# Where TensorE's operands begin in SBUF: a two-block transformer forward pass, dense activations placed 256 bytes past the weights

## The chip, the cores and the metric

The kernel runs on one core of one Trainium2 chip. The metric is the device time of one execution in microseconds. Three executions of the kernel before took 2189.39, 2189.68 and 2189.95 us, so the median is 2189.68 us.

## What is computed

Two blocks, one after the other, on 256 tokens of width 1024, all in float32. The first has two layers (a mixer with four branches, then a dense SwiGLU in layer 0 and a mixture of eight experts in layer 1). The second has two hybrid layers (retention, a state-space mixer, stick-breaking attention, a memory read). What matters for the change is the matrix products, which are nearly all of TensorE's work:

```python
z = rms_norm(h, norm1_g) @ w_in[layer]            # 256x1024 @ 1024x7168, cut into branches and gates
merged = sum(gates[i] * (y[i] @ w_branch[i]) for i in range(4))
h = h + merged @ w_out[layer]
h = h + (silu(g) * u) @ w_down                    # layer 0: g, u = hn @ w_gate_up (d_ff 2816)
h = h + sum(combine[:, e] * swiglu(hn, w_gate_up[e], w_down[e]) for e in range(8))   # layer 1: d_ff 3584
# second block, per layer
proj = rmsnorm(x, pre_g) @ w_in_2[l]              # 1024 x 6664
kv = rmsnorm(mem, mem_norm_g) @ w_mem_kv[l]
x = x + rmsnorm(concat([y_ret, y_ssd, y_sb, y_mem]) @ w_out_2[l], post_g)
```

## The kernel before, in words

Every large product is made of three products in a rounded float32 format (fp32r). Weights and activations are each split into a high part (a rounded copy, made by ScalarE) and a low part (the remainder, made by VectorE). TensorE adds up activation-high x weight-high, activation-low x weight-high and activation-high x weight-low in one PSUM bank.

A TensorE product takes two instructions. LDWEIGHTS loads one operand into the array, always 128 columns wide here (8 for one narrow tile). MATMUL then streams the other operand past it, 512 or 256 columns wide. In this text they are the loaded and the streamed operand. TensorE starts the LDWEIGHTS of the next product while the present one streams.

The SBUF tensors that the products read:

- `ring`: 5 x 16 KB per partition. In the dense stages it is used as nine half tiles (`halves_r`) of 8 KB for weights, with `xT_low` in the last 8 KB. In the expert stage it holds five tiles of expert weights, and their low parts are written over them (`w_low`).
- `xT` / `xT_high`, `xT_low`: the transposed, normalised activations, eight chunks of 128 rows x 256 tokens. In the expert stage `xg_high`, the 128 tokens gathered for an expert, lies in `xT`'s memory.
- `arena`: one large tensor that three sets of views cut up in turn (`Views` objects A and B for the first block, E for the experts, C for the second block). In it lie `w_high`, `hid_high`, `hid_low`, `xg_low`, `hidT_*`, the branch outputs `ya_*` to `yd_*`, and in the second block `mg*`, the memory's activations, and `yT_high`, `yr_low`, `yd_low`, `ys_low`.

`weigh` (in the TensorE program) issues a dense product tile by tile. Its two forms are `rows` (L908), which loads 128 tokens of the activations and streams 512 columns of weights (256 in a few tiles), and `cols` (L914), which loads 128 columns of weights and streams 256 tokens:

```python
return pe.matmul(o[:, a:a + n], x[:, c, b * P:(b + 1) * P], w[:, k, col:col + n], **flags)   # L908, rows
return pe.matmul(o[:, a:a + SEQ], w[:, k, j * P:(j + 1) * P], x[:, c, :], **flags)           # L914, cols
```

The first of the two tensors is the loaded one. In a high half it alternates `high` and `low` activations; in the low half it takes `high` alone. The experts (L1169, L1170, L1173 for the up products, L1210, L1212, L1217 for the down products) load activations and stream 512 columns of `w_high` or `w_low`. L1147 and L1148 put an expert's last rows back. L955 transposes 128x128 blocks with the identity in `consts`. L1244 is the narrow tile: it loads 8 columns of weights and streams 256 tokens.

All chunks, blocks and column groups of these tensors are steps of 512 bytes or multiples of it (128 floats), the narrow tile's 32-byte steps excepted. So the place of an operand within 512 bytes is the place of its tensor's start, whichever chunk is read.

The order of the work is written out by hand in each engine's program. SyncE loads weights in the order in which TensorE needs them: each load waits until TensorE has finished with the piece of the ring that it overwrites (L827 for dense halves, L818 for expert tiles).

Of the kernel before, what the change touches and what calls it, by code (L numbers as in the profile page):

```python
# [17 lines left out]
P = 128  # L18
SEQ, D = 256, 1024
TB = SEQ // P  # L20
KC = D // P
# [34 lines left out]
NRAW, NTOP = 5, 4  # L56
RAW_AT, TOP_AT = (6, 7, 2, 3, 4), (5, 0, 1, 8)
HALF = 2048
# [306 lines left out]
def kernel_program(nc, t):  # L365
# [28 lines left out]
    with ctx:  # L394
        def sb(name, shape, dt=F32):
            return ctx.enter_context(nc.sbuf_tensor(name, shape, dt))
# [4 lines left out]
        def placed(name, shape, dt=F32):  # L401

            at = -(-nc.sbuf_base // 32) * 32
            return sb(name, shape, dt), at

        def rounded(name, shape, at):

            return nc.alloc_sbuf_tensor_at(name, [P, *shape], F32R, offset=at)


        ring, ring_at = placed("ring", [P, NSLOT, TILE])
        raw = ring[:, :, :].rearrange("p a b -> p (a b)")
        halves_r = rounded("halves_r", [NRAW + NTOP, HALF], ring_at)
        xT_low = rounded("xT_low", [KC, SEQ], ring_at + 4 * (NRAW + NTOP) * HALF)
        h = sb("h", [P, TB, D])
        xs, xs_at = placed("xs", [P, TB, D])
        ym_low = rounded("ym_low", [4, SEQ], xs_at + 4 * D)
        xT, xT_at = placed("xT", [P, KC, SEQ])
        xT_high = rounded("xT_high", [KC, SEQ], xT_at)
        consts = sb("consts", [P, 7, P])  # L420
        ident, flip, le, lt, ge, ones, slots_row = (consts[:, k, :] for k in range(7))
        ssq = sb("ssq", [P, 8])
        rstd = sb("rstd", [P, 8])
        par_all = sb("par_all", [P, LAYERS, 80])
        ARENA = 25400
        arena, arena_at = placed("arena", [P, ARENA])

        class Views:


            def __init__(self, at=0):
                self.at = at

            def __call__(self, *shape):
                n = math.prod(shape)
                v = arena[:, self.at:self.at + n]
                self.at += n
                assert self.at <= ARENA, self.at
                return shaped(v, *shape)

        def shaped(v, *shape):
            if len(shape) == 1:
                return v
            names = "abcd"[:len(shape)]
            return v.rearrange(f"p ({' '.join(names)}) -> p {' '.join(names)}",
                               **{k: s for k, s in zip(names[1:], shape[1:])})
# [23 lines left out]
        A = Views()  # L470
# [31 lines left out]
        branch_top = rounded("branch_top", [2 * WIDE], arena_at + 4 * A.at)  # L502
        sguT = A(4, P)
        zT = A(2, SEQ + 2)
        A(4)
        q_n = A(TB, ATTN)
        yd_high = rounded("yd_high", [HEADS, SEQ], arena_at + 4 * A.at)
        k_n = A(TB, ATTN)
# [53 lines left out]
        xg_high = rounded("xg_high", [KC, P], xT_at)  # L562
        rt = Views(ARENA - 256)(256)
        lt_r, ones_r, chosen_r = xg_low[:, 0, :], xg_low[:, 1, :], xg_low[:, 2, 0:2 * EXPERTS]
        flag_word = rt[0:1, 200:201].bitcast(I32)
        token_ids = rounded("token_ids", [TB, 8], arena_at + 4 * (ARENA - 256 + 176))
        next_rows = rt[:, 192:193].bitcast(U32)
# [3 lines left out]
        C = Views()  # L571
        mask_strict, mask_incl = C(TRI), C(TRI)
        rope_c, rope_s = C(TB, P), C(TB, P)
        decay = C(4, TRI)
        par = C(96)
        post_row = C(D)
        ssd_row = C(512)
        kmT = C(4, SEQ)
# [4 lines left out]
        gm = C(TB, 512)  # L583
        mg1_high = [rounded(f"mg1_high_{'ab'[k]}", [KC // 2, SEQ], arena_at + 4 * (C.at + k * KC // 2 * SEQ)) for k in range(2)]
        xbc = C(8, SEQ + 4)
        yd_low = rounded("yd_low", [4, SEQ], arena_at + 4 * C.at)
        xz = C(2 * TB, 512)
        xh, zs = xz[:, 0:TB, :], xz[:, TB:2 * TB, :]
# [10 lines left out]
        small2 = C(256)  # L599
        assert E.at <= ARENA - 256 and C.at <= E.at - 2 * KC * P  # L600

# [2454 lines left out]
```

## Time and profile before

| what | value |
|---|---|
| median of three runs | 2189.68 us |
| span of the profiled execution | 2188.4 us |
| time outside the span (median less span) | 1.3 us |
| TensorE MATMUL busy | 2150.1 us, 98% |
| LDWEIGHTS busy | 1812.1 us, 83% |
| VectorE, ScalarE, GpSimd busy | 73%, 61%, 4% |
| granted TensorE clock, mean | 0.996 of full speed |
| chain that ended last | TensorE 90%, VectorE 4%, DMA 3%, ScalarE 2% |

The span is the profiler's; no time of its own is known for the profiled execution beyond it, so its 2188.4 us stands beside the median. MATMULs overlap: the mean duration of one (some 390 ns for 512 columns) is longer than the step from one start to the next. The step is what costs time, and it is read from the chain of work: a piece of the chain with x48 matmuls in 10.91 us has a step of 10.91/48 = 227.3 ns.

### The profile page before, as it was taken

The numbers are of one execution on the slowest core, as the hardware profiler recorded it, in microseconds if no ns is written. First come the engines' busy times: TensorE is split into PE (matmuls) and PEld (weight loads), VectorE is DVE, ScalarE is ACT, GpSimd is POOL, SyncE is SP. The second block draws the span as 40 slices with busy tenths as digits, with TensorE's granted clock in tenths as the row PEclk, the third lists the DMA queues.
The fourth block names the chain that finished last, engine by engine and source line by source line (L and its number), as shares of the span: only waits on it lengthen the run. The fifth ranks groups of instructions, "written<-read, shape, count | busy, mean of one in ns | idle before, by whom it ended". The sixth has DMA issues, their size and how long they took to land.

```text
span 2188.4 us, 27831 instructions
## 1 busy us (share of the span) xinstructions
PE 2150.1 (98%) x10935; PEld 1812.1 (83%) x10935; DVE 1592.3 (73%) x1339; ACT 1331.8 (61%) x1151; POOL 78.0 (4%) x67
## 2 busy tenths in 40 slices
PE   7999999999998999999999999999999999999998
PEld 6988788888787888888888888888888898899987
DVE  5576555466766888888888888888896667565665
ACT  4475544455656677776777777777675555456542
POOL 3100000000000000000000000000110000000000
PEclk9999999999998999999999999999999999999999
DMA  8554565554538999999999999999996534455442
GB/s 279 156 191 147 208 201 177 183 183 155 198 139 310 335 383 375 370 375 372 386 364 381 375 377 365 382 375 370 384 374 225 173 117 153 157 178 173 134 154 77
DMA packets 249166, 569.70 MB, mean 260 GB/s; under 512 B 12169, under 2 KB 14353, under 8 KB 248817
## 3 DMA queue, kind: packets, MB, share of 16 engines
q1 hardware_dynamic: 242368, 546.41, 69.8%
q0 software_dynamic: 5136, 16.70, 2.3%
q10 hardware_dynamic: 1568, 5.31, 0.6%
q8 instruction: 64, 1.05, 0.2%
q14 instruction: 30, 0.24, 0.0%
HBM read 562.60 MB, written 5.78 MB: 260 GB/s over the span
## 4 chain that ended last, share of the span: by engine, by line
PE 90%; DVE 4%; DMA 3%; ACT 2%; issue 0%; SPq 0%; DVEq 0%; ACTq 0%
PE bank L908 32%; PE bank L1169 9%; PE bank L1170 9%; PE bank L1173 9%; PE bank L914 9%; PE bank L1217 5%; PE bank L1210 5%; PE bank L1212 5%; PE bank L955 3%; DMA ring<-w_in 2%; DVE halves_r L2185 1%; DMA ring<-moe_w_down 1%; ACT halves_r L1663 1%; DVE w_low L2613 0%; DMA ring<-w_out 0%
## 5 line engine op out<-in xcount | busy, mean ns | idle before, releaser
L2613 DVE TENSOR_TENSOR w_low<-ring,w_high 128x4096 fp32r<-128x4096 f32 x167 | 736.3, 4421 | 75.8 <-ACT w_high L1892 75.1
L1892 ACT ACTIVATE w_high<-ring 128x4096 fp32r<-128x4096 f32 x167 | 606.8, 3634 | 236.5 <-DMA ring<-moe_w_gate_up 141.4
L908 PE MATMUL bank<-halves_r,xT_high 128*128 128x512 f32 (+1 forms) x1856 | 563.3, 381 | 6.1 <-ACT halves_r L1663 3.1
L2185 DVE TENSOR_TENSOR halves_r<-ring,halves_r 128x2048 fp32r<-128x2048 f32 x175 | 391.6, 2265 | 162.2 <-ACT halves_r L1663 160.0
L908 PEld LDWEIGHTS bank<-halves_r,xT_high 128*128 128x128 f32 x1856 | 344.1, 189 | 73.8 <-issue 5.2
L1663 ACT ACTIVATE halves_r<-ring 128x2048 fp32r<-128x2048 f32 x175 | 326.2, 1891 | 118.7 <-DMA ring<-w_in 55.5
L1169 PE MATMUL bank<-w_high,xg_high 128*128 128x512 f32 x896 | 357.6, 399 | 1.7 <-DVE xg_low L2590 1.7
L1170 PE MATMUL bank<-w_high,xg_low 128*128 128x512 f32 x896 | 351.8, 393 | 0.0
L908 PE MATMUL bank<-halves_r,xT_low 128*128 128x512 f32 (+1 forms) x928 | 348.7, 380 | 0.0
L1173 PE MATMUL bank<-w_low,xg_high 128*128 128x512 f32 x896 | 224.3, 392 | 0.0
L908 PEld LDWEIGHTS bank<-halves_r,xT_low 128*128 128x128 f32 x928 | 175.3, 189 | 32.1
L1169 PEld LDWEIGHTS bank<-w_high,xg_high 128*128 128x128 f32 x896 | 168.3, 188 | 38.5 <-issue 1.9
L1173 PEld LDWEIGHTS bank<-w_low,xg_high 128*128 128x128 f32 x896 | 168.2, 188 | 37.9
L1170 PEld LDWEIGHTS bank<-w_high,xg_low 128*128 128x128 f32 x896 | 168.5, 188 | 35.8
L1210 PE MATMUL bank<-w_high,hid_high 128*128 128x512 f32 x448 | 176.6, 394 | 0.0
L1212 PE MATMUL bank<-w_high,hid_low 128*128 128x512 f32 x448 | 174.9, 390 | 0.0
L914 PE MATMUL bank<-xT_high,halves_r 128*128 128x256 f32 x896 | 165.1, 284 | 0.0
L1641 ACT ACTIVATE arena<-bank 128x512 f32<-128x512 f32 x82 | 47.4, 596 | 158.0 <-PE bank L914 82.3
L914 PEld LDWEIGHTS bank<-xT_high,halves_r 128*128 128x128 f32 x896 | 140.9, 192 | 0.9 <-issue 0.8
L1217 PE MATMUL bank<-w_low,hid_high 128*128 128x512 f32 x448 | 114.2, 394 | 0.4 <-DVE w_low L2613 0.4
L914 PE MATMUL bank<-xT_low,halves_r 128*128 128x256 f32 x448 | 108.8, 283 | 0.0
L1217 PEld LDWEIGHTS bank<-w_low,hid_high 128*128 128x128 f32 x448 | 84.0, 188 | 20.0 <-DVE w_low L2613 0.8
(392 smaller groups left out, 2312.7 us busy)
## 6 DMA issues: line engine op xcount, KB each, us to landing
ring<-moe_w_gate_up SPq DMA_DIRECT2D x224, 1024.0 KB, 10.4
ring<-moe_w_down SPq DMA_DIRECT2D x112, 1024.0 KB, 9.8
ring<-w_in SPq DMA_DIRECT2D x108, 1024.0 KB, 5.2
ring<-w_out SPq DMA_DIRECT2D x24, 1024.0 KB, 4.9
ring<-ffn_w_gate_up SPq DMA_DIRECT2D x22, 1024.0 KB, 5.3
ring<-ffn_w_down SPq DMA_DIRECT2D x11, 1024.0 KB, 4.8
ring<-w_mem_kv SPq DMA_DIRECT2D x8, 1024.0 KB, 5.1
ring<-w_branch_attn SPq DMA_DIRECT2D x4, 1024.0 KB, 5.1
```

Of the source, the lines that this page charges most:

```text
L908: return pe.matmul(o[:, a:a + n], x[:, c, b * P:(b + 1) * P], w[:, k, col:col + n], **flags)
L914: return pe.matmul(o[:, a:a + SEQ], w[:, k, j * P:(j + 1) * P], x[:, c, :], **flags)
L1169: pe.matmul(o[:, :], xg_high[:, c, :], w[:, c, :], start=c == 0, stop=False)
L1170: pe.matmul(o[:, :], xg_low[:, c, :], w[:, c, :], start=False, stop=False)
L1173: mm = pe.matmul(o[:, :], xg_high[:, c, :], w[:, c, :], start=False, stop=c == KC - 1)
L1210: pe.matmul(acc[n][:, :], hid_high[:, 4 * k + c, :], v[:, c, :], start=k + c == 0, stop=False)
L1212: pe.matmul(acc[n][:, :], hid_low[:, 4 * k + c, :], v[:, c, :], start=False, stop=False)
L1217: mm = pe.matmul(acc[n][:, :], hid_high[:, 4 * k + c, :], v[:, c, :], start=False, stop=4 * k + c == EX_CH - 1)
L1663: act.activation(top_view(half), raw_view(half), ACT.Copy).then_inc(top_in, 1)
L1892: act.activation(high_slot(k), ring[:, ring_r.slot(names[k]), :], ACT.Copy).then_inc(w_high_in[r], 1)
L2185: dve.tensor_tensor(raw_view(half, halves_r), raw_view(half), top_view(half).bitcast(F32), ALU.subtract).then_inc(raw_low_in, 1)
L2613: dve.tensor_tensor(w_low[:, slot, :], ring[:, slot, :], high_slot(k).bitcast(F32), ALU.subtract).then_inc(w_low_in[r], 1)
```

## The change

It changes where tensors begin in SBUF, and nothing else. Each engine issues the same instructions on the same shapes, in the same order and with the same waits as before; only addresses differ. The allocation order changes (the arena now comes before `ssq`, `rstd` and `par_all`), two fillers of 256 bytes are put in, the arena shrinks by 56 floats, and three views of the arena are rounded up to a multiple of 128 floats.

Start of each tensor in bytes, modulo 512:

| tensor | before | after |
|---|---|---|
| `halves_r`, `w_low` (ring), `consts` | 128 | 128 |
| `xT_low`, `xT_high`, `xg_high`, `xs`, `ym_low` | 128 | 384 |
| `w_high`, `hid_high`, `hid_low`, `xg_low`, `hidT_high`, `hidT_low` | 320 | 128 |
| `ya_*`, `yb_*`, `yc_*`, `branch_top` | 320 | 128 |
| `yd_high`, `yd_lower` (first block) | 352 | 128 |
| `mg*` of the second block's layer 0 / layer 1 | 320 / 192 | 128 |
| `yT_high`, `yr_low`, `yd_low`, `ys_low` | 320 | 128 |

The distance of a product is here the start of the operand that is being loaded less the start of the one that is being streamed, modulo 512. Distances, before and after:

| streamed, loaded during it | line | before | after |
|---|---|---|---|
| `halves_r`, `xT_*` | L908 | 0 | 256 |
| `xT_*`, `halves_r` | L914 | 0 | 256 |
| `halves_r`, `hidT_*`, `yT_high` and three of the four low parts of y | L908 | 192 | 0 |
| `halves_r`, `mg*` of layer 0 / 1 | L908 | 192 / 64 | 0 |
| `mg*` of layer 0 / 1, `halves_r` | L914 | 320 / 448 | 0 |
| `w_high`, `xg_low` | L1169 | 0 | 0 |
| `w_high`, `xg_high` | L1170 | 320 | 256 |
| `w_low`, `xg_high` | L1173 | 0 | 256 |
| `w_high`, `hid_*` | L1210, L1212 | 0 | 0 |
| `w_low`, `hid_high` | L1217 | 192 | 0 |

```diff
@@ -411,25 +411,32 @@
-        xT_low = rounded("xT_low", [KC, SEQ], ring_at + 4 * (NRAW + NTOP) * HALF)
+        xT_low = rounded("xT_low", [KC, SEQ], ring_at + 4 * (NRAW + NTOP) * HALF + 2 * P)
+        sb("xT_low_end", [P, P // 2])
...
         xT_high = rounded("xT_high", [KC, SEQ], xT_at)
+        sb("half_line", [P, P // 2])
         consts = sb("consts", [P, 7, P])
         ident, flip, le, lt, ge, ones, slots_row = (consts[:, k, :] for k in range(7))
+        ARENA = 25344
+        arena, arena_at = placed("arena", [P, ARENA])
         ssq = sb("ssq", [P, 8])
         rstd = sb("rstd", [P, 8])
         par_all = sb("par_all", [P, LAYERS, 80])
-        ARENA = 25400
-        arena, arena_at = placed("arena", [P, ARENA])
+        assert ring_at % (4 * P) == (xT_at + 2 * P) % (4 * P) == arena_at % (4 * P)
...
+            def line_up(self):
+
+                self.at = -(-self.at // P) * P
...
         zT = A(2, SEQ + 2)
-        A(4)
+        A.line_up()
         q_n = A(TB, ATTN)
...
         par = C(96)
+        C.line_up()
         post_row = C(D)
...
         xbc = C(8, SEQ + 4)
+        C.line_up()
         yd_low = rounded("yd_low", [4, SEQ], arena_at + 4 * C.at)
```

## Rows read from the trace of the kernel before

**Rows 1.** The page, part 1: busy time, share, instructions of TensorE's matmuls

```profile
PE 2150.1 (98%) x10935; PEld 1812.1 (83%) x10935; DVE 1592.3 (73%) x1339; ACT 1331.8 (61%) x1151; POOL 78.0 (4%) x67
```

**Rows 2.** The page, part 4: the chain that ended last, by engine

```profile
PE 90%; DVE 4%; DMA 3%; ACT 2%; issue 0%; SPq 0%; DVEq 0%; ACTq 0%
```

**Rows 3.** Waits of PE, longest; waits of SP on expert matmuls (us, times, longest)

```profile
PE bank L955 <- DVE xs L2170: 11.8, 4, 9.3
...
SPq L818 <- PE bank L1173: 506.1, 88, 15.5
...
SPq L818 <- PE bank L1217: 230.5, 44, 10.8
```

**Rows 4.** Windows: us, busy by engine with instructions, clock, DMA share, GB/s

```profile
1000.00:1300.00 300.00, 300.00 (x1353) 245.29 (x1352) 255.58 (x102) 219.92 (x103) 8.92 (x2) 1.00 0.99 374
1700.00:1950.00 250.00, 247.00 (x1485) 218.83 (x1484) 160.70 (x227) 133.65 (x190) 1.59 (x3) 1.00 0.49 161
```

**Rows 5.** Groups of instructions by line and shape: x count, busy us, mean ns

```profile
L908 PE MATMUL bank<-halves_r,xT_high 128*128 128x512 f32 x1664 | 526.8, 393 | 6.1 <-ACT halves_r L1663 3.1 <-DVE xT_low L2178 1.8 <-issue 0.9
L1169 PE MATMUL bank<-w_high,xg_high 128*128 128x512 f32 x896 | 357.6, 399 | 1.7 <-DVE xg_low L2590 1.7
...
L908 PE MATMUL bank<-halves_r,xT_low 128*128 128x512 f32 x832 | 325.3, 391 | 0.0
...
L1210 PE MATMUL bank<-w_high,hid_high 128*128 128x512 f32 x448 | 176.6, 394 | 0.0
...
L914 PE MATMUL bank<-xT_high,halves_r 128*128 128x256 f32 x896 | 165.1, 284 | 0.0
...
L914 PE MATMUL bank<-xT_low,halves_r 128*128 128x256 f32 x448 | 108.8, 283 | 0.0
...
L908 PE MATMUL bank<-halves_r,yT_high 128*128 128x512 f32 x256 | 81.5, 395 | 1.9 <-DVE yr_low L2798 1.9
...
L908 PE MATMUL bank<-halves_r,hidT_high 128*128 128x512 f32 x176 | 55.2, 392 | 0.0
...
L908 PE MATMUL bank<-halves_r,xT_high 128*128 128x256 f32 x192 | 36.6, 284 | 0.0
```

**Rows 6.** Timeline, expert stage: start us, us, engine (PEld is LDWEIGHTS)

```profile
1000.12 0.39 PE L1169 MATMUL bank<-w_high,xg_high 128*128 128x512 f32 x1
1000.12 0.19 PEld L1170 LDWEIGHTS bank<-w_high,xg_low 128*128 128x128 f32 x1
```

**Rows 7.** Chain pieces (start us, us, what), distance 0

```profile
307.82 21.81 PE bank L908 x96
...
463.57 10.91 PE bank L908 x48
...
1748.85 11.52 PE bank L914 x96
```

**Rows 8.** Chain pieces at other distances: hidT, then mg

```profile
387.90 46.72 PE bank L908 x204
...
1661.93 7.54 PE bank L914 x64
1669.47 5.60 PE bank L908 x24
...
1676.82 5.28 PE bank L908 x23
...
1931.70 5.60 PE bank L908 x24
```

**Rows 9.** Windows over two up tiles, then two down tiles, of one expert

```profile
998.88:1010.39 11.51, 11.51 (x54) 9.41 (x53) 9.96 (x4) 8.25 (x4) 0.00 (x0) 1.00 0.87 338
1010.39:1021.84 11.45, 11.45 (x54) 9.40 (x53) 11.34 (x6) 7.87 (x3) 0.00 (x0) 1.00 1.03 412
```

**Rows 10.** Chain pieces: the transposes inside one of these windows, the narrow tile

```profile
1004.43 0.44 PE bank L955 x4
...
1716.26 2.77 PE bank L1244 x24
```

## The prediction

> **What bounds the kernel now.** I read the busy shares first, then the chain that ended last, then TensorE's own waits. MATMULs are busy 2150.1 of 2188.4 us [rows 1], and the chain lies on TensorE for 90% [rows 2]. The longest wait of TensorE for anything is 11.8 us in total [rows 3], which is mostly the start of the program. So the time is the sum of the steps from one matmul to the next, about 10,900 of them, and an edit that moves no instruction can matter only through that step.
>
> The expert stage needs a second look, because the DMA engines are busy there too: share 0.99 at 374 GB/s, while TensorE has no idle microsecond in 300 [rows 4]. Who waits for whom settles it. SyncE's loads wait for expert matmuls to free a tile for 506.1 + 230.5 us [rows 3]. The loads are paced by TensorE there, not the other way round.
>
> **What the step depends on.** The granted clock is 1.00 in the windows read [rows 4], the 2.4 GHz level, at which 512 columns take 213.3 ns and 256 columns 106.7 ns. The steps are longer, and they differ with where the two operands begin:
>
> - distance 0, 512 columns: 21.81/96 = 227.2 ns and 10.91/48 = 227.3 ns; distance 0, 256 columns: 11.52/96 = 120.0 ns [rows 7]
> - distance 192, 512 columns: 46.72/204 = 229.0 ns in the down product of the dense SwiGLU; for the memory's activations 5.60/24 = 233.3 ns in one product and 5.28/23 = 229.6 ns in the next [rows 8]
> - distance 64, 512 columns: 5.60/24 = 233.3 ns, the piece at 1931.70 [rows 8]
> - distance 320, 256 columns: 7.54/64 = 117.8 ns [rows 8].
>
> The same instruction on the same shape thus takes 227 to 233 ns, depending on the place. A cause is at hand: the LDWEIGHTS of the next product starts with the MATMUL that is streaming (both at 1000.12) and runs 0.19 us of its step [rows 6]. It and the stream read SBUF side by side. The extra is 13.3 ns per product for 256 columns (120.0 less 106.7) and about 14 ns for 512, so it comes once per product and not per column, as it would if the load disturbs the stream.
>
> **The change part by part.** No engine gets an instruction more or less, nor a wait. There are three groups of products.
>
> *First, products that leave other distances for 0.* I price them at 227.3 ns, the step of 48 matmuls behind a break [rows 7].
>
> - Expert up products, 3 x 896 = 2688 (L1169, L1170 and L1173 have the same count [rows 5]). Two up tiles take 11.51 us less 0.44 for four transposes, over 48 matmuls: 230.6 ns [rows 9, 10]. Only a third of them (L1169) ends at distance 0, the rest at 256; see below.
> - Expert down products, 3 x 448 = 1344. Two tiles: (11.45 - 0.44)/48 = 229.4 ns [rows 9, 10]. At 227.3 they save 1344 x 2.1 = 2.8 us.
> - `yT_high` (256) with three low parts of 32 each, and `hidT` (176 high and half as many low): 352 + 264 = 616 at 229.0, saving 616 x 1.7 = 1.0 us [rows 5, 8].
> - `mg` under L908, 96 products, about three quarters of them at 233.3 and the rest at 229.6: 232.4 on the mean, saving 0.5 us. `mg` under L914, 192 products, goes the other way, from 117.8 to 120.0: plus 0.4 us [rows 7, 8].
>
> *Second, the dense products with `xT`*, which go from 0 to 256: 1664 + 832 = 2496 with 512 columns, and 896 + 448 + 192 + 96 = 1632 with 256 columns [rows 5] (the low half of the last pair has half the count of the high). No row shows distance 256. I bound it by the nearest rows. Above, 233.3 for 512 columns [rows 8] and 120.0 for 256 [rows 7]. Below, the narrow tile: 24 matmuls of 256 columns, at distances from 0 to 224 in steps of 32, take 2.77/24 = 115.4 ns with only 8 columns to load [rows 10]; that is 4.6 ns under 120.0, and I put the same 4.6 under 227.3 for a low end of 222.7. The clock allows no less than 106.7 and 213.3.
>
> I take no change for this group: 227.3 and 120.0. The reason is the pattern of the distances. 320 is 64 plus 256, and the distances 192 and 64, also 128 apart, share the value 233.3 [rows 8]. If the places repeat every 128 or 256 bytes, 256 is the same as 0.
>
> *Third, the two thirds of the expert up products that end at 256.* By the same assumption all 2688 fall from 230.6 to 227.3: 8.9 us.
>
> VectorE, ScalarE and the DMAs also read and write at new places. TensorE does not wait for them by more than a microsecond or two at a time, so a few nanoseconds per instruction stay hidden; if they grew until the experts' weights came late, a wait of TensorE on `w_low` would appear. The loads must run 230.6/227.3 = 1.4% faster in the up tiles, about 380 GB/s for 374, and a window here shows 412 [rows 4, 9].
>
> Sum: -8.9 - 2.8 - 1.0 - 0.5 + 0.4 = -12.8 us on a span of 2188.4, so 2175.6. The median lies 1.3 us above the span of the profiled execution, which makes 2176.9; I say 2177.
>
> **A rule against it.** The Trainium skill (TensorE: Matmul & The Clock Gate, Part 2, on LDWEIGHTS) says that TensorE has two independent SBUF read ports, so that loading the next weights takes no read bandwidth from the running matmul, and SBUF — State Buffer, in its summary of who contends, says TensorE never waits on anyone. By that rule placement does nothing and the sum is 0. The trace does not agree: one shape has steps of 227.3, 229.0 and 233.3 ns.
>
> **The rivals.**
>
> *A half-line distance frees the stream.* If the places repeat every 512 bytes, 256 is the farthest that two starts can be apart, and it may be better than 0. For it: 256 columns run faster at 320 (117.8) than at 0 (120.0). Against it: 512 columns do not, at 192 or 64. Price at the low ends: 2496 x 4.6 = 11.5 us, 1632 x 4.6 = 7.5 us, and 1792 expert products from 227.3 to 222.7, 8.2 us, beyond the 12.8: -40.0 us, 2149.7. At the clock's own floor it would be 34.9 + 21.7 + 25.1 us beyond it, 2095; the expert loads would then hardly keep up.
>
> *Distance 256 is one of the bad ones; slower.* The mechanism is that of the 233.3 ns products: the dense `rows` products (L908) leave the good distance 0. 2496 x 6.0 = +15.0 us; 1632 x -2.2 = -3.6 us; 1792 expert up products from 230.6 to 233.3, +4.8; the other 896 to 227.3, -3.0; the rest -3.9. Together +9.3 us, 2199.0. For it: every distance other than 0 that a row shows for 512 columns is worse than 0. Against it: none of those is 256. It decides from a step of about 231.1 ns for these 4288 products: there 2496 x 3.8 + 1792 x 0.5 = 10.4 us, which is what the other terms save. At 229.0, the commoner value of distance 192, the sum is still -9.2 us.
>
> *The start places do nothing.* The steps of 229 and 233 ns might come from what other engines and DMAs do in those stages, not from the place; the time would stay 2189.7. The rule of the Trainium skill above would end there too. For it: the slow up products stand where the DMA share is 0.99. Against it: the `mg` products of both layers repeat 5.60 us to the hundredth, 262 us apart, and the dense product at 387.90 holds 229.0 over 204 matmuls while its neighbours hold 227.2.
>
> **How the numbers follow.** The forecast (256 acts like 0, or near the 229.0 case) gets 0.42, the gain at half a line 0.27, the slower case 0.20, no effect 0.11. A measurement of this kernel can tell 0.2%, 4.4 us, from no change. Faster: 0.42 + 0.27, less a little for weak versions of the forecast that stay within 4.4 us: 0.67. Same: 0.13. Slower: 0.20. The likeliest case alone spans 2172 to 2183. For 8 in 10 the range must take in the middle of the half-line rival below and nearly all of the slower one above: 2146 to 2200.
>
> **What would show it.** In the changed profile, TensorE stays at 98% with the same 10,935 matmuls. Pieces of the chain over dense `rows` products of x48 should still take 10.91 us and `cols` of x96 11.52 us; 10.69 or less means the half-line rival, 11.2 the slower one. The `hidT` piece of x204 should fall from 46.72 to about 46.4 us. Two expert down tiles should take 11.35 us for 11.45. The forecast fails if the dense pieces move either way, since 4128 products depend on one distance that no row shows; it also fails if a wait of TensorE on `w_high` or `w_low` of more than 2 us in total turns up.

## The result, and the profile after

The changed kernel takes 2178.36 us (median of four, 2178.17 to 2178.79). The kernel before, run beside it on the same chip, takes 2189.81 us. The ratio is 0.9942, with a 95% interval from 0.9928 to 0.9955, so the kernel is 11.4 us or 0.6% faster. The forecast was 2177.0.

The page, parts 1 and 4, of the kernel after: busy time with share and instructions, then the chain that ended last by engine. It stands against [rows 1, 2].

```profile
PE 2137.2 (98%) x10935; PEld 1811.7 (83%) x10935; DVE 1591.8 (73%) x1339; ACT 1331.9 (61%) x1151; POOL 78.2 (4%) x67
...
PE 90%; DVE 4%; DMA 3%; ACT 2%; issue 0%; SPq 0%; DVEq 0%; ACTq 0%
```

The matmuls are busy for 12.9 us less with the same count, and no other engine's busy time moved by more than 0.5 us. The chain's shares are the same. The span fell by 11.8 us, from 2188.4 to 2176.6.

Waits in the kernel after: engine, line, what was waited for, us in total, times, longest. They stand against [rows 3].

```profile
PE bank L964 <- DVE xs L2179: 12.4, 4, 9.4
...
PE bank L1226 <- DVE w_low L2622: 0.6, 1, 0.6
...
SPq L827 <- PE bank L1182: 493.1, 88, 15.8
...
SPq L827 <- PE bank L1226: 228.9, 44, 11.3
```

TensorE's own long wait is 0.6 us longer, and its wait on expert weights is 0.6 us in all. SyncE's waits for the expert matmuls fell by 13.0 + 1.6 us, since TensorE frees the tiles earlier.

Windows of the kernel after: two up tiles, two down tiles, and 300 us of the expert stage, with the columns of [rows 4]. They stand against [rows 9] and the first line of [rows 4].

```profile
994.24:1005.61 11.37, 11.37 (x53) 9.40 (x53) 9.96 (x4) 8.33 (x4) 0.00 (x0) 1.00 0.92 346
1005.61:1016.98 11.37, 11.37 (x53) 9.42 (x53) 11.20 (x6) 7.89 (x3) 0.00 (x0) 1.00 1.03 415
1000.00:1300.00 300.00, 300.00 (x1367) 247.79 (x1366) 258.05 (x103) 222.65 (x104) 12.94 (x3) 1.00 1.01 378
```

In the same 300 us TensorE starts 1367 matmuls where it started 1353, that is 1.0% more, and the loads run at 378 GB/s for 374. Two tiles of 48 products with four transposes (0.44 us, as in [rows 10]) take 11.37 us: (11.37 - 0.44)/48 = 227.7 ns a step, for 230.6 and 229.4 before.

Pieces of the chain of the kernel after (start us, us, what), against [rows 7, 8, 10]: dense products with `xT` (twice x96), `hidT` (x204), `xT` again (x48), the `mg` products (from 1650.82 to 1665.71), the narrow tile (1705.11) and 256-column products with `xT` (1737.70).

```profile
306.82 21.78 PE bank L917 x96
329.48 21.81 PE bank L917 x96
386.78 46.30 PE bank L917 x204
462.31 10.93 PE bank L917 x48
...
1650.82 7.67 PE bank L923 x64
1658.50 5.47 PE bank L917 x24
...
1665.71 5.46 PE bank L917 x24
...
1705.11 2.77 PE bank L1253 x24
...
1737.70 11.52 PE bank L923 x96
```

The pieces that went from distance 0 to 256 did not move: 21.81 and 21.78 for 21.81, 10.93 for 10.91, 11.52 for 11.52. Those that went from another distance to 0 did: 46.72 to 46.30 over 204 products (229.0 to 227.0 ns), 5.60 to 5.47 over 24 (233.3 to 227.9), and, the other way, 7.54 to 7.67 over 64 products of 256 columns (117.8 to 119.8).

Added up over the whole trace by kind of product, the difference is as below. A step is the time from the start of one matmul to the start of the next and is counted for the first of the two. The sums are made from the records of both traces. The means leave out steps over 300 ns, which have a wait or transposes in them; the sums keep them.

| products | mean step before, ns | after | sum, us |
|---|---|---|---|
| up, `w_high` x `xg_high`, 896 | 231.7 | 227.9 | -3.10 |
| up, `w_high` x `xg_low`, 896 | 230.5 | 228.0 | -2.27 |
| up, `w_low` x `xg_high`, 896 | 230.0 | 227.0 | -2.66 |
| down, `w_low` x `hid_high`, 448 | 231.8 | 227.3 | -1.36 |
| down, the other 896 | 228.3 | 227.3 | -0.37 |
| `yT` with its low parts, `hidT`, `mg` rows, 712 | 229.3 | 227.1 | -1.53 |
| first block's `ya` to `yd`, 240 | 231.7 | 228.7 | -0.61 |
| `mg` cols, 192 of 256 columns | 126.1 | 128.1 | +0.24 |
| dense with `xT`, 2496 of 512 columns | 227.4 | 227.2 | -1.05 |
| everything else, transposes above all | | | +0.83 |

Together that is -11.9 us, and the span fell by 11.8. (The means of the `mg` cols have short breaks in them; inside their pieces the step goes from 117.8 to 120.0.)

The down products lost part of their gain again. Their steps under 300 ns alone save (231.8 - 227.3) x 444 = 2.0 us and 1.0 ns x 875 = 0.9 us. Of the steps over 300 ns there are 28 for 22, and they took 1.2 us more than the others' pace would give. One of the new ones took 230 ns before and takes 382 ns now. The timeline of the kernel after at that place (start us, us, engine, line, and in brackets the idle time ahead with its releaser):

```profile
1511.60 3.63 ACT L1901 ACTIVATE w_high<-ring 128x4096 fp32r<-128x4096 f32 x1 [0.89 <-DMA ring<-moe_w_gate_up]
...
1515.52 0.19 PEld L1219 LDWEIGHTS bank<-w_high,hid_high 128*128 128x128 f32 x1 [0.41 <-ACT w_high L1901]
1515.52 0.49 PE L1219 MATMUL bank<-w_high,hid_high 128*128 128x512 f32 x1
```

ScalarE waited 0.89 us for the weights from memory, its rounded copy came late, and the load that TensorE could have done beside the last stream had to wait for it. The faster matmuls have reached the weight stream at a few tiles.

The waits of TensorE's weight loads on the experts' rounded weights, before and then after (us in total, times, longest), show the same:

```profile
PEld bank L1210 <- ACT w_high L1892: 1.3, 5, 0.3
...
PEld bank L1217 <- DVE w_low L2613: 0.8, 1, 0.8
```

```profile
PEld bank L1219 <- ACT w_high L1901: 2.0, 6, 0.4
...
PEld bank L1226 <- DVE w_low L2622: 1.0, 1, 1.0
```

With one more of 0.2 us in the up products, these are 3.2 us after for 2.1 us before. Part of each is hidden under the stream of the product ahead.

### The profile page after: what moved, and what is told of

Its sections match the earlier page's. It is cut to its first block, busy times and chain, and to the rows that moved or that the text cites. A ratio compares the mean times of both kernels' runs of the same rounds, so it can differ in the third digit from the quotient of the medians.

```text
span 2176.6 us, 27831 instructions
## 1 busy us (share of the span) xinstructions
PE 2137.2 (98%) x10935; PEld 1811.7 (83%) x10935; DVE 1591.8 (73%) x1339; ACT 1331.9 (61%) x1151; POOL 78.2 (4%) x67
## 3 DMA queue, kind: packets, MB, share of 16 engines
q8 instruction: 64, 1.05, 0.2%
## 4 chain that ended last, share of the span: by engine, by line
PE 90%; DVE 4%; DMA 3%; ACT 2%; issue 0%; SPq 0%; DVEq 0%; ACTq 0%
PE bank L917 33%; PE bank L1178 9%; PE bank L1179 9%; PE bank L1182 9%; PE bank L923 9%; PE bank L1226 5%; PE bank L1219 5%; PE bank L1221 5%; PE bank L964 3%; DMA ring<-w_in 2%; DVE halves_r L2194 1%; DMA ring<-moe_w_down 1%; ACT halves_r L1672 1%; DVE w_low L2622 0%; DMA ring<-w_out 0%
## 5 line engine op out<-in xcount | busy, mean ns | idle before, releaser
L1672 ACT ACTIVATE halves_r<-ring 128x2048 fp32r<-128x2048 f32 x175 | 326.2, 1892 | 118.6 <-DMA ring<-w_in 57.4
L1219 PEld LDWEIGHTS bank<-w_high,hid_high 128*128 128x128 f32 x448 | 84.1, 188 | 19.2 <-ACT w_high L1901 2.0
## 6 DMA issues: line engine op xcount, KB each, us to landing
ring<-moe_w_gate_up SPq DMA_DIRECT2D x224, 1024.0 KB, 10.6
```

Source lines behind the costliest of these rows:

```text
L1219: pe.matmul(acc[n][:, :], hid_high[:, 4 * k + c, :], v[:, c, :], start=k + c == 0, stop=False)
L1672: act.activation(top_view(half), raw_view(half), ACT.Copy).then_inc(top_in, 1)
```

## The experiments

All kernels were run beside the kernel before, and each ratio is against that one. The edits are given against the kernel after, except that of `only_xt`, which is given against the kernel before; the changes to the closing assert that go with them are left out. The first four ask what the shift of `xT` by 256 bytes does, the next four give `xT` other distances, and the last three move all operands together, the arena alone, or `xT_low` alone.

**all_same: the activations at the same place as the weights.** No filler, so that every distance named in the table of the change is 0.

```diff
-        xT_low = rounded("xT_low", [KC, SEQ], ring_at + 4 * (NRAW + NTOP) * HALF + 2 * P)
-        sb("xT_low_end", [P, P // 2])
+        xT_low = rounded("xT_low", [KC, SEQ], ring_at + 4 * (NRAW + NTOP) * HALF + 0)
...
-        sb("half_line", [P, P // 2])
```

> All TensorE operands begin at the same place within 512 bytes: xT, xT_low and xg_high at distance 0 from the weights instead of 256, the arena lined up as in the changed kernel. Theory R (places repeat every 256 bytes or less, and the gain comes from the products that left 192, 320 and 64): the same time as the changed kernel, 2178.4 us within 1 us; dense 512-column pieces of x48 at 10.91 us, 256-column pieces of x96 at 11.52 us. Rival H (256 is itself a good distance and part of the gain hangs on it): slower than the changed kernel, by up to the 3.5 us that the xT products and the half of the up products reading xg_high contributed.

Measured: 2181.04 us (2180.28 to 2182.87), ratio 0.9958 (0.9942 to 0.9975). The span is 2178.0 us. Pieces of its chain: dense rows, `hidT`, dense cols.

```profile
283.86 21.77 PE bank L915 x96
...
386.47 46.30 PE bank L915 x204
...
1739.19 11.52 PE bank L921 x96
```

These are the pieces of the kernel after within 0.01 us. The medians differ by 2.7 us, but they come from different chips, so both kernels were timed again on one.

**after_again and all_same_again.** The two kernels unchanged, on one chip together.

> The changed kernel once more, beside all_same_again on one chip. If 0 and 256 are alike the two agree within 0.1%, 2 us; if 256 is the better of the two, this one is faster by 1 to 3 us, as the first pair of medians (2178.4 and 2181.0, on different chips) could suggest.

> All operands at distance 0, beside after_again: the same time within 2 us if 0 and 256 are alike; slower by 1 to 3 us if the half line is worth something of its own.

Measured: after 2179.03 us (2177.95 to 2182.61), ratio 0.9948 (0.9935 to 0.9962); all at the same place 2178.36 us (2177.36 to 2180.78), ratio 0.9944 (0.9930 to 0.9957). The 2.7 us are gone, and the sign with them. The shift by 256 bytes, which the change is named after, is worth nothing that these runs can tell from 0; lining up the rest, which is all that the kernel with everything at one place does, is worth all of it.

**only_xt: the shift alone.** Against the kernel before, with the arena's start where it was modulo 512 and no view rounded up.

```diff
-        xT_low = rounded("xT_low", [KC, SEQ], ring_at + 4 * (NRAW + NTOP) * HALF)
+        xT_low = rounded("xT_low", [KC, SEQ], ring_at + 4 * (NRAW + NTOP) * HALF + 2 * P)
+        sb("xT_low_end", [P, P // 2])
...
+        sb("half_line", [P, P // 2])
...
-        ARENA = 25400
+        ARENA = 25360
```

> The kernel before with one part of the change alone: xT, xT_low and xg_high moved from 0 to 256 bytes past the weights; the arena's tensors keep their places (320, 352, 192). Theory R: no change, 2189.8 us within 1 us, since 0 and 256 are alike, and so are 320 and 64 for L1170. Rival H: part or all of the 11.4 us is here, down to 2178 us.

Measured: 2190.23 us for 2190.28 before, ratio 1.0003 (0.9993 to 1.0012). Its chain and its window of the expert stage:

```profile
307.23 21.81 PE bank L910 x96
...
387.31 46.72 PE bank L910 x204
...
1747.91 11.52 PE bank L916 x96
```

```profile
1000.00:1300.00 300.00, 300.00 (x1353) 245.30 (x1352) 255.75 (x101) 219.93 (x103) 8.92 (x2) 1.00 0.99 374
```

All three pieces and the 1353 matmuls are those of before [rows 4, 7, 8]. Here the up products go from distance 320 to 64 and from 0 to 256, and the dense ones from 0 to 256; no step moves.

**xt_128: the activations 128 bytes on.** If the places repeated every 128 bytes, this would be the kernel after again.

```diff
-        xT_low = rounded("xT_low", [KC, SEQ], ring_at + 4 * (NRAW + NTOP) * HALF + 2 * P)
-        sb("xT_low_end", [P, P // 2])
+        xT_low = rounded("xT_low", [KC, SEQ], ring_at + 4 * (NRAW + NTOP) * HALF + 128)
+        sb("xT_low_end", [P, 32])
...
-        sb("half_line", [P, P // 2])
+        sb("half_line", [P, 96])
```

> As the changed kernel, but xT, xT_low and xg_high are 128 bytes past the weights instead of 256. If places repeat every 128 bytes: 2178.4 us within 1 us. If they repeat only every 256 bytes, 128 is a distance that no row has shown, and it may be as bad as 64: 2496 dense and 1792 expert products at 229.0 to 233.3 ns instead of 227.2, that is +8 to +26 us, less 3.6 us for 1632 products of 256 columns at 117.8 ns: 2183 to 2201 us.

Measured: 2201.03 us (2199.95 to 2202.58), ratio 1.0048 (1.0032 to 1.0065): 23 us above the kernel after. Dense rows, `hidT`, dense cols:

```profile
287.26 22.30 PE bank L917 x96
...
391.63 46.30 PE bank L917 x204
...
1756.82 11.39 PE bank L923 x96
```

The dense product with `xT` takes 232.3 ns a step, while `hidT`, whose distance is still 0, stays at 227.0 in the same trace. So the slower step belongs to the operands and not to the run. A period of 128 bytes is out.

**xt_64, xt_320 and xt_32.** The same edit with 64, 320 and 32 bytes, each with fillers that keep all else where it is. 64 and 320 are 256 apart.

```diff
-        xT_low = rounded("xT_low", [KC, SEQ], ring_at + 4 * (NRAW + NTOP) * HALF + 2 * P)
+        xT_low = rounded("xT_low", [KC, SEQ], ring_at + 4 * (NRAW + NTOP) * HALF + 320)   # or 64, 32
```

> As the changed kernel, but xT, xT_low and xg_high are 64 bytes past the weights. The distance theory: 512-column products with xT settle at 233.3 ns, as those of mg at distance 64 did, or walk 226, 229, 232 at 229.0 as those at 192 did; 4288 products x 1.8 to 6.1 ns = +8 to +26 us, and 1632 products of 256 columns go from 120.0 to 117.8 ns, -3.6 us: 2183 to 2201 us, and I take 2195. Rival (what made steps longer in the kernel before was not the distance but the stage or the arena's own place): 2178.4 us.

> As the changed kernel, but xT, xT_low and xg_high are 320 bytes past the weights. If places repeat every 256 bytes this is xt_64 over again: 2196 us within 2 us, dense 512-column products at 233.3 ns on the mean and 256-column ones at 113.6 or 117.8. If they repeat every 512 bytes it is a distance of its own, and the two need not agree in either.

> As the changed kernel, but xT, xT_low and xg_high are 32 bytes past the weights. If the cost grows with the distance up to 128: between all_same and xt_64, 2185 to 2193 us. If any distance other than a multiple of 256 breaks the settled step at once: 4288 products at 232 to 234 ns, +21 to +29 us, less some 3 us of the 256-column ones: 2197 to 2206 us. I take the second.

Measured: at 64, 2195.95 us, ratio 1.0021 (1.0012 to 1.0031); at 320, 2196.73 us, ratio 1.0026 (1.0015 to 1.0036); at 32, 2203.36 us, ratio 1.0059 (1.0042 to 1.0076). The profiled execution at 64 took 10.6 us more than the median, so the rows at 320 are read first: dense rows, `hidT`, one dense product behind a break, then the cols.

```profile
286.82 22.40 PE bank L917 x96
...
391.18 46.29 PE bank L917 x204
...
467.10 11.21 PE bank L917 x48
...
1687.96 22.61 PE bank L923 x192
```

Products of 512 columns take 22.40/96 = 233.3 ns, those of 256 columns 22.61/192 = 117.8 ns for 120.0. The two signs are those of [rows 8], now in products that had distance 0 there. 64 and 320 give the same time within 0.05%, and in the trace at 64 the same three kinds of piece take 22.40, 46.29 and 22.61 us, as at 320. So places that are 256 bytes apart are alike here too. The rows at 32 bytes, dense rows and then cols:

```profile
286.86 22.40 PE bank L917 x96
...
1694.45 22.40 PE bank L923 x192
```

The 512-column piece takes 22.40 us here as well, so a small distance does as much harm as a large one. The 256-column products gain most here: 22.40/192 = 116.7 ns.

**whole_64: everything 64 bytes on.** All distances are 0, and only the place of all operands together changes, from 128 to 192 within 512.

```diff
+        sb("front", [P, 16])
...
-        xT_low = rounded("xT_low", [KC, SEQ], ring_at + 4 * (NRAW + NTOP) * HALF + 2 * P)
-        sb("xT_low_end", [P, P // 2])
+        xT_low = rounded("xT_low", [KC, SEQ], ring_at + 4 * (NRAW + NTOP) * HALF + 0)
...
-        sb("half_line", [P, P // 2])
```

> All operands at distance 0 as in the run all_same, but the whole of SBUF's tensors begins 64 bytes further on (192 within 512 instead of 128). If only the distance counts: the time of all_same, 2181 us within 1.5 us, and the same steps of 226.7 and 120.0 ns. Rival (the place itself counts, the distance is a stand-in for it): the dense products move by several ns, 2190 us or more.

Measured: 2180.53 us (2178.89 to 2182.65), ratio 0.9953 (0.9937 to 0.9970).

```profile
284.32 21.77 PE bank L916 x96
...
386.92 46.29 PE bank L916 x204
...
1737.81 11.52 PE bank L922 x96
```

Same steps, same time within the interval. Of the two places tried, neither is better by itself; the distance between the two operands decides.

**arena_64: the arena 64 bytes on, the rest at one place.** `w_high`, `hid_*`, `xg_low`, `hidT_*`, `yT_high` and `mg*` move together against ring and `xT`. This gives the arena's operands a distance again, with all else as in the kernel with all at one place.

```diff
-        xT_low = rounded("xT_low", [KC, SEQ], ring_at + 4 * (NRAW + NTOP) * HALF + 2 * P)
-        sb("xT_low_end", [P, P // 2])
+        xT_low = rounded("xT_low", [KC, SEQ], ring_at + 4 * (NRAW + NTOP) * HALF + 0)
...
-        sb("half_line", [P, P // 2])
...
+        sb("arena_from", [P, 16])
```

> As all_same, but the arena begins 64 bytes further on within 512 than ring and xT: dense xT products stay at distance 0, L1217, hidT and the y and mg products go to 64, L1170 to 448. Distance theory: L1217 448 x 6.0 = 2.7 us, hidT and y 616 x 6.1 = 3.8 us, mg 0.6 us less 0.4 to 1.2 us of its 256-column products, and the pair L1169, L1170 back at about 231 ns as at 0 and 320, 1792 x 3.9 = 7.0 us: +13 us on all_same, 2194 us, with L1169's and L1170's group bearing half of it. Rival (the experts' steps were set by DMA and engine traffic, not by distance): those two stay at 227.2 and the sum is +7 us, 2188.

Measured: 2196.19 us (2193.55 to 2197.93), ratio 1.0018 (1.0009 to 1.0028), 15 us above the kernel with all at one place. Dense `xT`, then `hidT`, then the last eight products of an up tile and of a down tile:

```profile
284.86 21.79 PE bank L916 x96
...
387.80 47.59 PE bank L916 x204
...
986.70 1.84 PE bank L1181 x8
...
1015.25 1.87 PE bank L1225 x8
```

Now it is `hidT` that is slow, 47.59/204 = 233.3 ns, and `xT` is not: the reverse of the rows at 128 and 320. The eight down products at 1.87 us (233.8 ns) load `hid_high` from the arena and stream `w_low` from the ring. The eight up products at 1.84 us (230.0 ns; 1.81 or 1.82 in the kernel after) are the odd ones: they load from `xT` and stream from the ring, at distance 0, but each such row of eight comes behind products with `w_high`, half of which have a distance other than 0. Over all 672 such products that have one of their own kind ahead of them and behind them, the mean step is 230.5 ns for 226.7. So a product's step depends also on what came before it. The kernel before shows the same: these 672 products are at distance 0 there too and take 230.1 ns, and with `xT` at 256 alone (`only_xt`) they take 230.3.

`hidT` also shows that a distance and its mirror image differ. At 192 (the kernel before) its steps, read from the starts in the trace, walk 226, 229 and 232 ns in turn, 229.0 on the mean; at 64 (this run) they alternate between 231 and 236 ns, 233.3 on the mean.

**low_64: `xT_low` alone 64 bytes on.** In a high half the dense products alternate between `xT_high` (distance 0) and `xT_low` (distance 64).

```diff
-        xT_low = rounded("xT_low", [KC, SEQ], ring_at + 4 * (NRAW + NTOP) * HALF + 2 * P)
-        sb("xT_low_end", [P, P // 2])
+        xT_low = rounded("xT_low", [KC, SEQ], ring_at + 4 * (NRAW + NTOP) * HALF + 64)
+        sb("xT_low_end", [P, 16])
...
+        sb("to_line", [P, 112])
...
-        sb("half_line", [P, P // 2])
```

> As all_same, but xT_low alone begins 64 bytes further on; xT_high, xg_high and the arena stay at distance 0. In a high half the products alternate, so only every second load is at distance 64. If each step hangs on its own pair alone: 832 steps at 233.3, the others at 226.7, +5.5 us, less up to 5 us of the 256-column products: 2179 to 2187. If the step carries over to the next one, as the pair at 0 and 320 in the kernel before suggests (230.5 and 231.7, both long), 1664 steps at about 231: +6.5 us, less 2.5 us for the 256-column ones: 2185 us, and both members of a pair are longer.

Measured: 2184.42 us (2181.68 to 2187.22), ratio 0.9967 (0.9955 to 0.9978).

```profile
285.26 22.01 PE bank L917 x96
...
1743.02 11.39 PE bank L923 x96
```

The piece of 96 stands between 21.77 and 22.40. In the high halves the step of a product with `xT_low` is 231.9 ns (827 steps) and that of one with `xT_high` 229.7 (701, those between two with `xT_low`), for 227.2 each with all at one place; in the low halves, where `xT_low` is not read, it is 227.5 for 226.7 (650). The load of `xT_low` runs beside the stream of the `xT_high` product, but the longer of the two steps is the next one, that of the product whose own loaded operand is off.

No experiment beats the changed kernel. The version with all at one place equals it and needs two fillers of 256 bytes less. Not tried: weights at distance 0 for the `rows` products and at 64 for the `cols` products, which the rows at 320 price at 1344 x 2.2 ns = 3 us of gain for those with `xT`. It would need an operand at two places, and whether SBUF has room for that was not worked out.

## Why the prediction was right, and where it was not

*TensorE's steps are the time.* Right. The products whose operands moved account for 12.7 us of the steps, everything else gave 0.8 us back, and the span fell by 11.8. None of the waits of TensorE's matmuls shown moved by more than 0.6 us. The forecast of 2177 was 1.4 us low: 1.0 us of it lies in the span (2175.6 forecast, 2176.6 measured), the rest in the time outside it, taken as 1.3 us and measured as 1.8.

*The step depends on the places of the two operands.* Shown: `xT` slow and `hidT` not at 128 and 320, `hidT` slow and `xT` not with the arena moved, on the same instructions. The rival that placement does nothing is out. By the Trainium skill (TensorE: Matmul & The Clock Gate, Part 2) a weight load takes no SBUF read bandwidth from the running matmul. If that made placement free, as the prediction's rival had it, the runs do not agree: one `hidT` product takes 227.0 or 233.3 ns a step over 204 matmuls, by the place of the arena alone.

*256 acts like 0 for the 4128 products with `xT`.* Right, and measured three times: the shift alone (ratio 1.0003), the two kernels side by side (0.9948 and 0.9944), and 64 against 320 (1.0021 and 1.0026). The prediction left open whether places repeat every 128 or 256 bytes. It is 256: at 128 the kernel is slower than before. The reason given for it was weaker than the result, and that part of the hit is luck. That 192 and 64 "share the value 233.3" spoke as much for 128 as for 256, and had the change used 128 the same reasoning would have missed by 24 us. Nor do they share it in long pieces: `hidT` has 229.0 at 192 and 233.3 at 64. And the row at 320 was of 256 columns, those at 64 and 192 of 512, so they could not be compared.

*Up products, -8.9 us.* Measured -8.0. The steps fell to 227.0 with `w_low` but to 227.9 and 228.0 with `w_high`, where 227.3 was taken for all three. The price was right and the reason given covers only a part of it. Two of the three kinds (L1169 and L1173) were at distance 0 before, by the table of the change. By distance alone they would have had 227.3 ns already, and only the 896 products of L1170 had something to gain: 5.4 us even if they had stood at 233.3. The prediction took the mean of 230.6 from the trace, which held the carry-over that `arena_64` shows later, without asking why products at distance 0 should have it. Priced by distance, the term would have come out at least 2.6 us short of the measured one.

*Down products, -2.8 us.* Measured -1.7 as a sum, but -2.9 in the steps under 300 ns. The mean of 229.4 taken from one pair of tiles [rows 9] holds for the whole: (448 x 231.8 + 896 x 228.3)/1344 = 229.5. What the prediction did not price is the 1.2 us that came back in steps over 300 ns, at least in part where `w_high` was late for a step or two. It had put the bound for a failure at 2 us of TensorE's waits on these weights. The waits of the matmuls stayed below, at 0.6 us; those of the loads came to 3.2 us, but they were at 2.1 before the change, so the bound did not say which was meant. The two down tiles took 11.37 us for 11.35 forecast.

*`yT`, `hidT`, `mg`, together -1.1 us.* Measured -1.3: -1.53 for the 712 products of 512 columns and +0.24 for the 192 of 256. The `hidT` piece came to 46.30 us for 46.4. The sum left out the 240 products of the first block's branches (`ya` to `yd`), 80 of which stream `halves_r` and leave 192 or 224 for 0 as well; they saved 0.6 us more, 0.4 of it in those 80.

*Dense products with `xT`, 0.* Measured -1.1 us over 2496 products of 512 columns, 0.4 ns each. Not explained. It is not the shift: where `xT_high` and `xT_low` alternate, the kernel with the shift alone has 227.6 ns, as before, and the one with all at one place 227.2. With the arena alone moved to 64 it is 227.6 again. Inside the low halves all of these have 226.7 or 226.8. So it comes with the arena's lines; whether it is a carry-over from the arena's products was not tested.

*The gain at half a line, 0.27, and the slower case, 0.20.* Neither came. The dense and down products of 512 columns at distance 0 or 256 settle at 226.7 to 227.3 ns, the up products at 227.0 to 228.0; no group came near the 222.7 of that rival. The slower case was the right price for another distance: 2199.0 forecast for a bad one, 2201.0, 2196.7 and 2203.4 measured at 128, 320 and 32.

*What causes it.* The prediction named the load that runs beside the stream, with an extra that comes once per product. Three findings fit it only in part. The product after the disturbed stream is the longer one. Products at distance 0 behind others stay at 230.5 ns. And a distance other than 0 makes 512-column products slower but 256-column ones faster, which an extra per load does not give. The narrow tile, which loads 8 columns, keeps 115.4 ns a step in both kernels [rows 10], less than the 120.0 of a full load at distance 0; but its distance changes with each product, and full loads reach 116.7 at distance 32, so how far a smaller load helps is open. That load and stream meet at one place in SBUF is argued and not shown; what the runs show is the dependence on the distance.

## What to carry to other kernels

When TensorE is the bound and every product has its own load, write down for each pair of loaded and streamed operand the difference of their starts modulo 256 bytes, and bring it to 0 for 512-column products. For fp32r products with a load of 128 columns that was worth 1 to 6 ns in 230 a product here, and 11 us in all, for a few fillers. Line up all products of a tile, since one kind at another distance slows its neighbours too. Price such an edit from the steps between starts in the chain, not from mean durations, and over all tiles of a kind rather than over one pair. Don't read the name of the change as its cause: the shift that gives this one its name did nothing, and the lining up beside it did everything.

## What the runs showed of the hardware

- The step of a 512-column fp32r product with its own 128-column load is 226.7 to 227.3 ns at distance 0 or 256 when its neighbours are there too (up to 228.0 in the up products). It is 232 to 233.3 ns in dense pieces at 32, 64, 128 and 320, at a granted clock of 1.00 in the windows read (the 2.4 GHz level). At 192 `hidT` lay between, with 229.0 [rows 8].
- For 256 columns the sign turns: 120.0 ns at distance 0 and 256, 117.8 at 320, and 116.7 at 32. At 128 the piece shown has 118.6 (11.39/96), and the mean over all such products with `xT` is 119.0.
- The period is 256 bytes and not 128: 0 and 256 are alike, 64 and 320 are alike, 128 is not like 0. A distance and its mirror are not alike: `hidT` has 229.0 at 192 and 233.3 at 64.
- The distance counts and not the place: all operands at 128 or all at 192 within 512 bytes give the same steps.
- The effect outlasts its cause: in the expert up tiles, products at distance 0 run at 230.5 ns for 226.7 when products at another distance come ahead of them in the same tile.
